# A row's addition ahead of the squares of the row above, the last group's first rows in pairs, and layer 3's second root first: three reorderings in a three-layer network

## The chip, the core and the metric

The kernel runs on 1 core of a Trainium2 chip. Its engines work side by side and meet through semaphores: TensorE (PE; PEld is its weight load), VectorE (DVE), ScalarE (ACT), GpSimd (POOL) and SyncE (SP), which here only issues DMAs. The metric is the device time of one execution in microseconds (us), median over runs; lower is better.

## The reference

Three blocks follow one another on a sequence of 1024 positions with 1024 features, all in float32. The change lies where the second block ends and the third begins:

```python
# end of block 2 (its residual stream is h, DEPTH = 1)
n2 = rms_norm(h, ffn_norm_g)
up = causal_depthwise_conv(n2 @ w_ffn_up, ffn_conv_w, ffn_conv_b)   # 2 x 2816 columns
g, val = up[..., :D_FF_2], up[..., D_FF_2:]
h = h + (jax.nn.silu(g) * val) @ w_ffn_down                          # 2816 -> 1024
h = rms_norm(h, final_norm_g)
# start of block 3
z = rmsnorm(x, pre_g) @ w_in                                         # x is that h; z has v, u, gate, q, k, ...
# end of block 3
x + rmsnorm(y, post_g)
```

`rms_norm(x, g)` is x * rsqrt(mean(x^2) + 1e-6) * g over the features. So two norms with two gains stand between the down product and layer 3's input product.

## The kernel before

**Layout.** Features lie on the 128 partitions, in eight rows (chunks) of 128 features; a row is 128 x 1024. The residual stream is `res` (`k.real(m)` is row m of it). Every large product is made in three matmuls per 128x128 weight block and 512 (or 342) columns: high parts, high times low, low times high (lines 263 to 265 in `product`, 296 to 298 in `three`). An operand therefore exists twice, as `x_hi` (rounded by ScalarE) and `x_lo` (the rest, by VectorE).

**Weights.** They come in the order in which TensorE wants them, in tiles of eight blocks (512 KB). Three buffers each: SP loads `w_raw` (a load waits until POOL is done with the tile three back), ScalarE rounds it to `w_hi` (`cast`, up to three tiles ahead of the tiles TensorE is done with; a cast waits for its load and for the buffer), POOL makes `w_lo` in four quarters, each of which counts `w_ready` up. A row of the down product is four blocks with two pieces of 512 columns, 24 matmuls; two rows use up one tile. A layer 3 product is eight blocks, one tile, 48 matmuls.

**Banks.** `claim` gives a product of two pieces one of two pairs of PSUM banks in turn, and TensorE waits until the reader of the product before in that pair has freed it. Banks 4 to 7 hold sums over partitions.

**Layer 2's MLP (`Ffn2`).** Hidden rows j = 0 to 21 are made by VectorE and ScalarE from the up products (two per j) and kept in a ring of five. The down product runs in groups of hidden rows `ks`: two, then five times four. In the last group `ks` is 18 to 21, and hidden row 21 is the last thing made before it. For each of the eight output rows m the kernel does, in the last group:

- TensorE: the product ("down", 5, m), all chunks of piece 0, then all of piece 1;
- VectorE: adds it to row m of `res` (frees the banks);
- ScalarE: two squares of the row, plain and with the gain (`self.square`), both into one pair of buffers (for m = 0 into the running sums `conv` themselves), so that squares m wait for the running sums of m - 1; then `x_hi` of the row;
- VectorE: adds the two squares to the running sums `conv` (`self.total`; in the profile `up_conv`), then makes `x_lo` of the row (`x3_ready`).

VectorE's order is by hand: addition m, sums m, `x_lo` m, addition m + 1. Behind the last row TensorE sums `conv` over the partitions (the moments, four products of float32 into banks 4 to 7).

**Layer 3's start (`Mixer3`).** From the moments come two roots, each of them guessed by ScalarE (`root_guess`: Ln, then Exp, with table loads) and refined by VectorE (`root_newton`: four dependent operations): `rms`, of layer 2's final norm, and `rms2`, of layer 3's norm, which is then multiplied by `rms`. VectorE's order in `dve` is: first root, two operations for the second root's input (`scale_ready`), eight scalings of `res` by the final gain and `rms` (`x_scaled`), second root, and then the products. ScalarE starts the second guess after the first scaled row. SP's order in `sp`: one small load, wait for eight `x_scaled`, the spill of `res` to DRAM (4 MB; block 3 needs it at its end), wait for it, two loads of 512 KB into the room of `res`, then the next weight tiles. The products v3 0 to v3 7 (values of the spatial gate) run on TensorE right behind the moments; VectorE multiplies each by `rms2` into `mix` (`dve_products`), which frees the banks. Every such multiplication stands behind the wait for the spill. ScalarE applies Gelu to each, and VectorE adds each to a running total one product later (`dve_v_total`), which waits for that Gelu. Six tiles of layer 3 are loaded before SP reaches the wait for the scalings; the first one behind the spill is that of v3 6.

The profile names helper lines: L96 is `tt` (two tensors), L102 `ts`, L105 `stt` (tensor, scalar, tensor), L124 `act`, L129 `copy` (casts), L136 `mm`, L140 `dma`. `work` holds the roots, `mix` the v3 products.

Of the kernel before, what the change touches and what calls it, by code (L numbers as in the profile page):

```python
# [7 lines left out]
P = 128  # L8
S = 1024
# [8 lines left out]
BLOCKS = 8  # L18
# [141 lines left out]
def halves_of(t):  # L160
    return t.rearrange("p (a b) -> p a b", a=2)
# [1844 lines left out]
class Ffn2:  # L2006
# [27 lines left out]
    def pe(self, t):  # L2034
        k = self.k
        for g, (js, ks) in enumerate(self.groups):
            for j in js:
                for i in range(2):
                    drain(k.product(t, ("up", j, i), [block_of("w_ffn_up_2", c, i * FF2 * P + j * P) for c in range(8)], k.hi, k.lo, FFN2,
                                    lambda c, _: [(self.mixer.n_ready, c + 1)]))  # L2040
            for m in range(8):
                drain(k.product(t, ("down", g, m), [block_of("w_ffn_down_2", c, m * P) for c in ks],
                                lambda c: self.h_hi[:, ks[c] % self.RING, :], lambda c: self.h_lo[:, ks[c] % self.RING, :], TWO,
                                lambda c, _: [(self.h_ready, ks[c] + 1)]))
        k.label("ffn 2")
        t.wait_ge(self.total, 14)
        t.mm(k.ones_of(self.conv[:, 0, :], TWO, (4, 5)), self.moments)
        t.mm(k.ones_of(self.conv[:, 1, :], TWO, (6, 7)), self.moments)

    def act(self, a):  # L2050
# [27 lines left out]
    def dve(self, v):  # L2078
# [7 lines left out]
        for g, (js, ks) in enumerate(self.groups):  # L2086
            last = g == len(self.groups) - 1
            for j in js:
# [17 lines left out]
                v.tt(self.h_lo[:, j % self.RING, :], self.conv[:, 0, :], self.h_hi[:, j % self.RING, :].bitcast(F32), ALU.subtract, inc=self.h_ready)  # L2106
            for m in range(8):
                p, x = k.products["down", g, m], k.real(m)
                v.wait_ge(*p.done)
                v.settle()  # L2110
                v.tt(halves_of(x), halves_of(x), k.view(p), ALU.add, inc=p)
                if not last:
                    continue
                v.wait_ge(self.square, 2 * m + 2)
                if m:
                    v.settle()
                    v.tt(self.conv[:, 0, :], self.conv[:, 0, :], self.up[:, 0, 0:S], ALU.add, inc=self.total)
                    v.tt(self.conv[:, 1, :], self.conv[:, 1, :], self.up[:, 1, 0:S], ALU.add, inc=self.total)
                v.wait_ge(self.x3_rounded, m + 1)
                v.stt(k.x_lo[:, m, 0:S], x, self.gains[:, m:m + 1], k.x_hi[:, m, 0:S].bitcast(F32), ALU.mult, ALU.subtract, inc=self.x3_ready)  # L2120


class Mixer3:
# [353 lines left out]
    def act(self, a):  # L2477
# [4 lines left out]
        k.root_guess(a, halves_of(self.rms), ps[:, 4:6, :], D, EPS, self.guess)  # L2482
        a.wait_ge(self.x_scaled, 1)
        k.root_guess(a, self.rms2, self.tmp, D, EPS, self.guess)
# [5 lines left out]
    def dve_products(self, v, name):  # L2490
        k = self.k
        for p in k.since(self.dve_at, name):
            n, i = p.key[0], p.key[-1]
            v.wait_ge(self.spilled, 16)
            v.wait_ge(*p.done)
# [16 lines left out]
            else:  # L2512
                out = self.g[i % 2]
            v.tt(halves_of(out)[rows], k.view(p, rows), halves_of(self.rms2)[rows], ALU.mult, inc=p)
            if n == "v3" and i:
                self.dve_v_total(v, i - 1)

    def dve_v_total(self, v, g):
# [179 lines left out]
    def dve(self, v):  # L2698
# [7 lines left out]
        v.tt(halves_of(self.tmp), ps[:, 6:8, :], halves_of(self.tmp), ALU.mult, inc=self.scale_ready)  # L2706
        for c in range(8):
            v.stt(k.real(c), k.real(c), k.column("final_norm_g_2", c), self.rms, ALU.mult, ALU.mult, inc=self.x_scaled)
        v.wait_ge(self.guess, 2)
# [314 lines left out]
```

## Time and profile before

| | |
|---|---|
| runs | median 3836.55 us of 3 (3836.2 to 3837.43) |
| profiled execution | 3839.78 us, of which the span from first to last instruction is 3838.0 |
| PE | 3533.0 us busy, 92% |
| DVE | 1763.2 us, 46% |
| ACT | 1121.9 us, 29% |
| POOL | 1064.7 us, 28% |
| chain that ended last | PE 80%, DVE 12%, ACT 5%, issue 2% |
| mean granted TensorE clock | 0.955 |

Busy time is summed over the span and can't tell which engine holds up a stage. The chain that ended last is followed back from the last instruction, at each step to what released it. The part of the trace that the change touches lies from about 2750 us (last up product) to about 2930 us (last v3 product) after the span's start.

### The profile page before, as it was taken

What the parts mean: (1) busy time and instruction counts of PE and PEld (TensorE: products, weight loads), DVE (VectorE), ACT (ScalarE), POOL (GpSimd) and SP (SyncE); (2) the same over time, 40 slices, a digit from 0 to 9 for tenths busy, and PEclk for the clock granted to TensorE, in tenths of its full rate; (3) what the DMA queues carried; (4) which work ended last, traced back from release to release, by engine and by line L of the source; (5) the groups of instructions that cost most, each with busy time, mean ns of one, the idle gap of its engine ahead of it and who ended that gap; (6) DMA issues with size and microseconds to landing.
All of it is one profiled execution on the core that took longest, in us unless ns stands there. A gap on an engine that the chain in (4) does not pass through costs nothing.

```text
span 3838.0 us, 39292 instructions
## 1 busy us (share of the span) xinstructions
PE 3533.0 (92%) x16326; PEld 2825.7 (74%) x16326; DVE 1763.2 (46%) x1823; ACT 1121.9 (29%) x1429; POOL 1064.7 (28%) x1136
## 2 busy tenths in 40 slices
PE   8988889999999688999998999999969899999987
PEld 6555667888887488555498989988856777777776
DVE  4566553222222668566456545544553322433433
ACT  3333242111112522434432111111232422322442
POOL 4111334323223233100023334433322122112243
PEclk9999999999999889899799999999989999999999
DMA  3000211111111111000021111111121111000232
GB/s 115 25 22 28 93 61 61 45 49 50 45 50 46 66 61 39 17 6 6 6 78 42 41 50 44 46 48 50 39 83 39 50 63 47 28 28 28 72 131 93
DMA packets 55961, 191.17 MB, mean 50 GB/s; under 512 B 6868, under 2 KB 7252, under 8 KB 55272
## 3 DMA queue, kind: packets, MB, share of 16 engines
q1 hardware_dynamic: 55784, 188.66, 14.5%
q8 instruction: 129, 2.11, 0.2%
q14 instruction: 48, 0.39, 0.0%
HBM read 171.78 MB, written 16.86 MB: 49 GB/s over the span
## 4 chain that ended last, share of the span: by engine, by line
PE 80%; DVE 12%; ACT 5%; issue 2%; DMA 0%; SPq 0%; DVEq 0%; ACTq 0%; POOL 0%; POOLq 0%
PE psum L263 21%; PE psum L265 21%; PE psum L264 21%; PE psum L136 13%; DVE work L96 2%; DVE res L96 2%; DVE res L105 1%; PE psum L296 1%; DVE mix L105 1%; ACT L124 1%; PE psum L298 1%; PE psum L297 1%; ACT res L124 1%; DVE work L114 1%; DVE u_padded L96 1%
## 5 line engine op out<-in xcount | busy, mean ns | idle before, releaser
L96 POOL TENSOR_TENSOR w_lo<-w_raw,w_hi 128x256 fp32r<-128x256 f32 x1132 | 1064.5, 971 | 2738.3 <-ACT w_hi L129 2738.3
L263 PE MATMUL psum<-x_hi,w_hi 128*128 128x512 f32 (+2 forms) x3416 | 1291.1, 378 | 76.9 <-DVE x_lo L96 22.4
L264 PE MATMUL psum<-x_lo,w_hi 128*128 128x512 f32 (+2 forms) x3416 | 1240.1, 363 | 0.0
L265 PE MATMUL psum<-x_hi,w_lo 128*128 128x512 f32 (+2 forms) x3416 | 1237.4, 362 | 0.0
L263 PEld LDWEIGHTS psum<-x_hi,w_hi 128*128 128x128 f32 x3416 | 651.1, 191 | 195.8 <-issue 55.7
L129 ACT CAST w_hi<-w_raw 128x1024 fp32r<-128x1024 f32 x283 | 296.8, 1050 | 1685.8 <-PE psum L265 1640.8
L264 PEld LDWEIGHTS psum<-x_lo,w_hi 128*128 128x128 f32 x3416 | 652.5, 191 | 95.1 <-issue 21.1
L265 PEld LDWEIGHTS psum<-x_hi,w_lo 128*128 128x128 f32 x3416 | 650.0, 190 | 82.6
L263 PE MATMUL psum<-h_hi,w_hi 128*128 128x512 f32 x864 | 345.8, 400 | 31.5 <-issue 10.4
L265 PE MATMUL psum<-h_hi,w_lo 128*128 128x512 f32 x864 | 343.6, 398 | 0.0
L264 PE MATMUL psum<-h_lo,w_hi 128*128 128x512 f32 x864 | 341.4, 395 | 0.0
L263 PEld LDWEIGHTS psum<-h_hi,w_hi 128*128 128x128 f32 x864 | 163.7, 190 | 75.5 <-issue 14.4
L105 DVE SCALAR_TENSOR_TENSOR res<-res,psum 128x1024 f32<-128x1024 f32 (+1 forms) x88 | 90.4, 1027 | 262.0 <-PE psum L265 248.1
L264 PEld LDWEIGHTS psum<-h_lo,w_hi 128*128 128x128 f32 x864 | 164.0, 190 | 40.3 <-issue 2.2
L265 PEld LDWEIGHTS psum<-h_hi,w_lo 128*128 128x128 f32 x864 | 163.9, 190 | 36.6
L136 PE MATMUL psum<-res 128*65 128x256 f32 (+5 forms) x480 | 179.1, 460 | 3.4 <-ACT work L124 3.1
L96 DVE TENSOR_TENSOR h_tmp<-h_tmp 128x1024 f32<-128x1024 f32 (+1 forms) x36 | 54.7, 1521 | 256.1 <-ACT h_tmp L124 256.1
L105 DVE SCALAR_TENSOR_TENSOR mix<-u_padded,vectors,mix 128x1044 f32<-128x1044 f32 x120 | 168.9, 1407 | 5.4 <-ACT work L129 1.2
L96 DVE TENSOR_TENSOR up<-psum,ffn_rms 128x1026 f32<-128x1026 f32 x44 | 54.0, 1227 | 201.6 <-PE psum L265 201.6
L105 DVE SCALAR_TENSOR_TENSOR up_conv<-up,vectors,up_conv 128x1024 f32<-128x1024 f32 x88 | 144.5, 1643 | 3.1
L96 DVE TENSOR_TENSOR res<-res,psum 128x1024 f32<-128x1024 f32 (+1 forms) x56 | 68.5, 1224 | 151.8 <-PE psum L265 150.4
L124 ACT ACT_TABLE_LOAD x100 | 128.3, 1283 | 7.2 <-PE psum L136 5.4
(254 smaller groups left out, 3432.8 us busy)
## 6 DMA issues: line engine op xcount, KB each, us to landing
w_raw<-w_dram SPq DMA_DIRECT2D x283, 512.0 KB, 3.3
res<-spill SPq DMA_DIRECT2D x4, 1044.0 KB, 8.7
res<-x_dram SPq DMA_DIRECT2D x8, 512.0 KB, 8.7
res<-x_dram SPq DMA_DIRECT2D x4, 1024.0 KB, 8.2
spill<-res SPq DMA_DIRECT2D x1, 4096.0 KB, 12.1
spill_a<-mix SPq DMA_DIRECT2D x8, 512.0 KB, 2.6
res<-spill_a SPq DMA_DIRECT2D x8, 512.0 KB, 4.9
x_plain<-spill SPq DMA_DIRECT2D x4, 1024.0 KB, 9.4
```

What stands on the lines that cost most here:

```text
L96: self.mark(self.e.tensor_tensor(out, a, b, op), inc)
L105: self.mark(self.e.scalar_tensor_tensor(out, a, s, b, op0, op1), inc)
L114: self.mark(self.e.reciprocal(out, a), inc)
L124: self.mark(self.e.activation(out, a, func, bias=bias, scale=scale), inc)
L129: self.mark(self.e.copy(out, a), inc)
L136: ins = self.e.matmul(out, lhsT, rhs, start=start, stop=stop, skip_group_check=True)
L263: t.e.matmul(out, whi, xhi, start=k == 0, stop=False, skip_group_check=True)
L264: t.e.matmul(out, whi, xlo, start=False, stop=False, skip_group_check=True)
L265: ins = t.e.matmul(out, wlo, xhi, start=False, stop=last_k, skip_group_check=True)
L296: t.e.matmul(out, whi, xhi, start=first, stop=False, skip_group_check=True)
L297: t.e.matmul(out, whi, xlo, start=False, stop=False, skip_group_check=True)
L298: return t.e.matmul(out, wlo, xhi, start=False, stop=last, skip_group_check=True)
```

## The change

In the last group of the down product rows 0 and 1 are computed together: chunks 18, 19 and 20 of row 0, the same of row 1, then chunk 21 of row 0 and of row 1, each block with both pieces; the weight blocks lie in this order in DRAM. VectorE adds row m + 1 to `res` before it waits for the squares of row m. In layer 3, ScalarE's second guess waits for its input only, not for the first scaled row; VectorE does four scalings, then the second root, then the products; scalings 4 to 7 follow the multiplications of v3 0 to 3, and the multiplications of v3 products don't wait for the spill.

```diff
@@ -2038,7 +2038,10 @@
                 for i in range(2):
                     drain(k.product(t, ("up", j, i), [block_of("w_ffn_up_2", c, i * FF2 * P + j * P) for c in range(8)], k.hi, k.lo, FFN2,
                                     lambda c, _: [(self.mixer.n_ready, c + 1)]))
-            for m in range(8):
+            last = g == len(self.groups) - 1
+            if last:
+                self.pe_first_two(t, g, ks)
+            for m in range(2 if last else 0, 8):
                 drain(k.product(t, ("down", g, m), [block_of("w_ffn_down_2", c, m * P) for c in ks],
                                 lambda c: self.h_hi[:, ks[c] % self.RING, :], lambda c: self.h_lo[:, ks[c] % self.RING, :], TWO,
                                 lambda c, _: [(self.h_ready, ks[c] + 1)]))
@@ -2046,6 +2049,27 @@
         t.wait_ge(self.total, 14)
         t.mm(k.ones_of(self.conv[:, 0, :], TWO, (4, 5)), self.moments)
         t.mm(k.ones_of(self.conv[:, 1, :], TWO, (6, 7)), self.moments)
+
+    def pe_first_two(self, t, g, ks):
+
+        k, products = self.k, []
+        tile, at = divmod(len(k.blocks), BLOCKS)
+        assert at == 0
+        order = [(m, c) for m in range(2) for c in range(3)] + [(m, 3) for m in range(2)]
+        k.blocks += [block_of("w_ffn_down_2", ks[c], m * P) for m, c in order]
+        for m in range(2):
+            p, before = k.claim(("down", g, m), 2, 512)
+            for stream, value in before:
+                t.wait_ge(stream, value)
+            products.append(p)
+        for n, (m, c) in enumerate(order):
+            t.wait_ge(k.w_ready, 4 * tile + n // 2 + 1)
+            t.wait_ge(self.h_ready, ks[c] + 1)
+            r, w = ks[c] % self.RING, (k.w_hi[tile % 3][:, n, :], k.w_lo[tile % 3][:, n, :])
+            for i, (t0, cols) in enumerate(TWO):
+                x = self.h_hi[:, r, t0:t0 + cols], self.h_lo[:, r, t0:t0 + cols]
+                ins = k.three(t, k.ps[:, products[m].first + i, :], w, x, c == 0, c == 3)
+            k.close(t, ins, products[m] if c == 3 else None, n == BLOCKS - 1)
 
     def act(self, a):
         k = self.k
@@ -2104,11 +2128,16 @@
                 v.tt(self.conv[:, 0, :], self.conv[:, 0, :], self.conv[:, 1, :], ALU.mult, inc=self.gated)
                 v.wait_ge(self.h_rounded, j + 1)
                 v.tt(self.h_lo[:, j % self.RING, :], self.conv[:, 0, :], self.h_hi[:, j % self.RING, :].bitcast(F32), ALU.subtract, inc=self.h_ready)
-            for m in range(8):
+            def add(m):
                 p, x = k.products["down", g, m], k.real(m)
                 v.wait_ge(*p.done)
                 v.settle()
                 v.tt(halves_of(x), halves_of(x), k.view(p), ALU.add, inc=p)
+
+            add(0)
+            for m in range(8):
+                if m < 7:
+                    add(m + 1)
                 if not last:
                     continue
                 v.wait_ge(self.square, 2 * m + 2)
@@ -2117,7 +2146,8 @@
                     v.tt(self.conv[:, 0, :], self.conv[:, 0, :], self.up[:, 0, 0:S], ALU.add, inc=self.total)
                     v.tt(self.conv[:, 1, :], self.conv[:, 1, :], self.up[:, 1, 0:S], ALU.add, inc=self.total)
                 v.wait_ge(self.x3_rounded, m + 1)
-                v.stt(k.x_lo[:, m, 0:S], x, self.gains[:, m:m + 1], k.x_hi[:, m, 0:S].bitcast(F32), ALU.mult, ALU.subtract, inc=self.x3_ready)
+                v.stt(k.x_lo[:, m, 0:S], k.real(m), self.gains[:, m:m + 1], k.x_hi[:, m, 0:S].bitcast(F32), ALU.mult, ALU.subtract,
+                      inc=self.x3_ready)
 
 
 class Mixer3:
@@ -2480,7 +2510,7 @@
         k.cast(a, k.at["ffn 2"][0])
         a.wait_ge(self.ffn.moments, 2)
         k.root_guess(a, halves_of(self.rms), ps[:, 4:6, :], D, EPS, self.guess)
-        a.wait_ge(self.x_scaled, 1)
+        a.wait_ge(self.scale_ready, 1)
         k.root_guess(a, self.rms2, self.tmp, D, EPS, self.guess)
         self.act_sgu(a)
         self.act_gla(a)
@@ -2491,7 +2521,8 @@
         k = self.k
         for p in k.since(self.dve_at, name):
             n, i = p.key[0], p.key[-1]
-            v.wait_ge(self.spilled, 16)
+            if n != "v3":
+                v.wait_ge(self.spilled, 16)
             v.wait_ge(*p.done)
             v.settle()
             rows = slice(0, 16) if n == "lr" else slice(0, P)
@@ -2512,8 +2543,15 @@
             else:
                 out = self.g[i % 2]
             v.tt(halves_of(out)[rows], k.view(p, rows), halves_of(self.rms2)[rows], ALU.mult, inc=p)
+            if n == "v3" and i < 4:
+                self.dve_normed(v, 4 + i)
             if n == "v3" and i:
                 self.dve_v_total(v, i - 1)
+
+    def dve_normed(self, v, c):
+
+        x = self.k.real(c)
+        v.stt(x, x, self.k.column("final_norm_g_2", c), self.rms, ALU.mult, ALU.mult, inc=self.x_scaled)
 
     def dve_v_total(self, v, g):
 
@@ -2704,8 +2742,8 @@
         v.tt(self.tmp, self.rms, self.rms, ALU.mult)
         v.settle()
         v.tt(halves_of(self.tmp), ps[:, 6:8, :], halves_of(self.tmp), ALU.mult, inc=self.scale_ready)
-        for c in range(8):
-            v.stt(k.real(c), k.real(c), k.column("final_norm_g_2", c), self.rms, ALU.mult, ALU.mult, inc=self.x_scaled)
+        for c in range(4):
+            self.dve_normed(v, c)
         v.wait_ge(self.guess, 2)
         v.settle()
         k.root_newton(v, self.rms2, self.W[3], self.tmp, D, EPS)
```

## Rows read from the trace of the kernel before

**Rows 1.** Waits of PE, whole span: who waited for whom, total, times, longest.
```profile
PE psum L263 <- DVE mix L96: 15.4, 3, 12.7
...
PE psum L136 <- DVE up_conv L96: 13.3, 1, 13.3
```
**Rows 2.** Timeline of PE, last down group: start, duration, what [idle before, releaser].
```profile
2759.16 0.79 PE L263 MATMUL psum<-h_hi,w_hi 128*128 128x512 f32 x1 [6.29 <-DVE h_lo L96]
...
2763.90 0.39 PE L265 MATMUL psum<-h_hi,w_lo 128*128 128x512 f32 x1
...
2775.24 0.39 PE L264 MATMUL psum<-h_lo,w_hi 128*128 128x512 f32 x1
...
2780.68 0.39 PE L264 MATMUL psum<-h_lo,w_hi 128*128 128x512 f32 x1
...
2793.26 0.50 PE L263 MATMUL psum<-h_hi,w_hi 128*128 128x512 f32 x1 [1.32 <-DVE res L96]
...
2819.89 5.56 PE L136 MATMUL psum<-up_conv,ones 128*128 128x512 f32 x8 [13.34 <-DVE up_conv L96]
```
**Rows 3.** Chain that ended last, down rows: start, duration, what.
```profile
2764.32 1.23 DVE res L96
...
2777.38 1.23 DVE res L96
2778.64 2.12 ACT up L124 x2
2780.78 2.36 DVE up_conv L96 x2
2783.14 1.69 DVE x_lo L105
2784.93 1.23 DVE res L96
```
**Rows 4.** Timeline of DVE, layer 3's start.
```profile
2835.92 11.10 DVE L105 SCALAR_TENSOR_TENSOR res<-res,vectors,work 128x1024 f32<-128x1024 f32 x8
2847.13 1.57 DVE L96 TENSOR_TENSOR work<-work 128x1024 f32<-128x1024 f32 x1
...
2850.72 2.48 DVE L96 TENSOR_TENSOR work<-work 128x1024 f32<-128x1024 f32 x2
2859.14 2.55 DVE L96 TENSOR_TENSOR mix<-psum,work 128x1024 f32<-128x1024 f32 x2 [5.93 <-DMA spill<-res]
```
**Rows 5.** DMA issues, 2835 to 2880: count, KB each, us to landing.
```profile
spill<-res SPq DMA_DIRECT2D x1, 4096.0 KB, 12.1
```
**Rows 6.** Stretch 2860.4 to 2865: length, busy (instructions) by engine, PEclk, DMA share, GB/s.
```profile
2860.40:2865.00 4.60, 4.58 (x12) 3.63 (x13) 1.23 (x1) 2.95 (x3) 2.47 (x4) 0.54 0.89 335
```
**Rows 7.** The scalings of `res` by form: duration ns min/median/max, first and last start.
```profile
L105 DVE SCALAR_TENSOR_TENSOR res<-res,vectors,work x8: 1275/1280/1771, 2835.9 to 2845.3; 128x1024 f32<-128x1024 f32 x8
```
**Rows 8.** Timeline of POOL, the tile made during the scalings.
```profile
2841.85 5.77 POOL L96 TENSOR_TENSOR w_lo<-w_raw,w_hi 128x256 fp32r<-128x256 f32 x4 [25.91 <-ACT w_hi L129]
```
**Rows 9.** Timeline of ACT, the second root's Ln and Exp.
```profile
2837.24 1.16 ACT L124 ACTIVATE work<-work,tiny 128x1024 f32<-128x1024 f32 x1 [6.95 <-DVE res L105]
...
2839.70 1.06 ACT L124 ACTIVATE work<-work 128x1024 f32<-128x1024 f32 x1
```
**Rows 10.** Timeline of DVE, two of the v3 multiplications.
```profile
2895.97 1.23 DVE L96 TENSOR_TENSOR mix<-psum,work 128x1024 f32<-128x1024 f32 x1 [8.04 <-PE psum L265]
...
2907.08 1.22 DVE L96 TENSOR_TENSOR mix<-psum,work 128x1024 f32<-128x1024 f32 x1 [8.04 <-PE psum L265]
```
**Rows 11.** Timeline of SP's queue, 2859 to 2960: the first weight loads behind the spill.
```profile
2860.00 99.65 SPq L140 DMA_DIRECT2D w_raw<-w_dram  x9
```
**Rows 12.** Tile `w_raw`, 2840 to 2900: duration ns min/median/max, first and last start; landing.
```profile
L96 POOL TENSOR_TENSOR w_lo<-w_raw,w_hi x19: 724/732/1717, 2841.8 to 2899.6; 128x256 fp32r<-128x256 f32 x19
L129 ACT CAST w_hi<-w_raw x5: 1027/1054/1054, 2840.7 to 2896.0; 128x1024 fp32r<-128x1024 f32 x5
...
DMA to landing us min/median/max: 3.2/3.3/5.5
```

## Prediction

> **What bounds the kernel now.** I read the waits of TensorE first. Of its matmuls' waits over the whole kernel, two large ones lie where the change is: 13.3 us ahead of the moment matmuls (`up_conv`), and 12.7 of the 15.4 us for `mix`, layer 3's first products [rows 1]. A third, 6.29 us for hidden row 21, stands in the timeline [rows 2]. So here TensorE isn't the limit; what VectorE does while it waits is the path.
>
> Then the timeline of TensorE in the last group of the down product. It restarts after the 6.29 us slowly: 14 steps from 2759.16 to 2763.90 take 4.74 us, where 24 steps from 2775.24 to 2780.68 take 5.44, 0.227 each, which would make 3.2 [rows 2]. These are the two levels of TensorE's clock.
>
> Then the chain, row by row [rows 3]. One period is addition (`res`) 2777.38, two squares on ScalarE 2778.64, two running sums (`up_conv`) 2780.78, `x_lo` 2783.14, next addition 2784.93: 7.55 us. No two of these overlap, since on VectorE the next addition stands behind sums that wait for the squares. The first addition is at 2764.32 [rows 3]; the moments start at 2819.89, after 13.34 us of idling [rows 2]. A row of products is 24 matmuls, 5.46 us, so TensorE is faster than the period and waits for banks (1.32 us at 2793.26) [rows 2].
>
> Then layer 3's start on VectorE: eight scalings in 11.10 us from 2835.92, the second root from 2847.13 to 2853.20 (2850.72 + 2.48), then idle until 2859.14, where the releaser is the spill [rows 4], a DMA of 12.1 us that SP issues behind the eighth scaling [rows 5]. Only then is product 0 read and TensorE let on, at 2860.4, again at the slow pace: 12 matmuls in 4.6 us [rows 6].
>
> **Part 1, rows 0 and 1 in pairs.** No matmul is added. Six (row, chunk) blocks need hidden rows 18 to 20 only: 36 matmuls, of which 9 ran before. The other 27 x 0.227 = 6.1 us go into the 6.29 us wait. TensorE still is held until 2759.16, but has hardly idled, so I take the full pace. Row 0 needs 6 more matmuls: last start 2760.30, and by the distance of before from last start to addition (2763.90 to 2764.32) its addition is at 2760.72 [rows 2, 3]. Row 1 follows 6 matmuls later, 2762.1. The price: row 2 takes row 0's banks and waits for addition 0 (1.23) until 2762.0, 0.1 us after row 1's last matmul.
>
> **Part 2, addition m+1 ahead of sums m.** No instruction is added, but the sums and `x_lo` of row m now stand behind VectorE's wait for product m+1, and the squares of row m+1 still wait for the sums of row m. VectorE's share of a row is 1.26 (addition) + 2.36 (sums) + 1.79 (`x_lo` with POOL beside it) = 5.4 us, 4.9 without POOL [rows 3, 7]. Squares and sums are 2.12 + 2.36 = 4.5. ScalarE has the squares, a third pass of about 1.1 and, every second row, a cast of 1.05: 4.3 at most [rows 3, 12]. All are below the 5.46 us of a row of matmuls. So the pace becomes TensorE's: row 2 starts at 2762.0, addition 2 comes at 2767.7, addition 7 at 2795.0. Behind it remain addition 7 (1.26), sums 6 (2.36, to 2798.65), squares 7 (2.12) and sums 7 (2.36): 2803.2. I allow 0.1 for POOL: moments at 2803.3, against 2819.89: **16.6 us**. Bounds: 16.9 with 5.44 per row; 14.9 if POOL slows the sums too (rival 2). TensorE still idles some 8 us ahead of the moments, so I leave them as slow as they are (5.56 us) [rows 2].
>
> Of POOL's part the trace shows that a scaling of 1.28 us becomes 1.77 while a tile of `w_lo` is made [rows 7, 8]. The Trainium skill (SBUF — State Buffer, "Who interferes with whom") says that a VectorE instruction with two SBUF inputs contends with a GpSimd instruction that reads SBUF, and that whichever is first holds the shared interface for its whole instruction. The trace agrees in kind. By the page both sums are exposed as `x_lo` is, and the addition, with one input in PSUM, is not: that is rival 2, and the sum would be 1.7 us smaller.
>
> **Part 3, layer 3.** Clock times are those of before. ScalarE's second guess waited for the first scaled row and starts at 2837.24; now it starts with `scale_ready`, about 2836.0. Its end, 2840.76 before (2839.70 + 1.06), becomes 2839.5 [rows 9], ahead of where VectorE asks for it. VectorE does four scalings at (11.10 - 3 x 1.69) / 5 = 1.2 us each [rows 4, 7], to 2840.8; three of the eight were slowed and lie 1.69 apart. Then the root, 6.07 us as before, to 2846.9. But the tile of POOL, 5.77 us from 2841.85 [rows 8], starts 1.2 us earlier too and now lies beside all of the root: three more operations with two SBUF inputs, at 0.35 to 0.49 each. I take 1.0, between none and 1.5: 2847.9. The multiplication of product 0 no longer waits for the spill and takes 1.23: TensorE goes on at 2849.2 instead of 2860.4: **11.2 us** (10.7 to 12.2). Its own work ended 12.7 before 2860.4 [rows 1], so the gap is 1.5 us. The 1.32 us gap of the down rows was not followed by a slow stretch (from 2793.26 to the next wait the row takes its 5.5 us), so the slow restart goes too: 12 matmuls at 0.227 are 2.7, not 4.6 us, **1.9 us** [rows 2, 6]. If the clock falls all the same, that 1.9 stays.
>
> The other four scalings follow multiplications 0 to 3, where VectorE idles 8.04 us per product [rows 10]: nothing. They hold no bank up: product 2 needs multiplication 0 alone.
>
> **Part 4, SP's queue.** SP holds, in order: the wait for all eight scalings, the spill, the wait for it, two loads of 512 KB, then the weights of product 6, which went out at 2860.00, 0.87 us after the spill had landed [rows 4, 11]. Products come every 11.11 us [rows 10]. From 2849.2 on, product 3 ends at 2871.4, its multiplication and the eighth scaling at 2874.1, the spill lands at 2886.2, the weight load goes out at 2887.0. It is behind two others, so I take the longest of the landings, 5.5 us, not the median of 3.3: 2892.5. Cast 1.05, the first quarter of POOL 0.73, 0.15 of handing over: 2894.4 [rows 12]. TensorE wants it 4 x 11.11 after 2849.2, at 2893.6. So a new stall of **0.8 us**; none with 3.3, 1.8 with POOL held up. Behind the late weights ScalarE's cast also holds up the activation of product 3, and so VectorE's running sum and the multiplication of product 5 by some 3 us, which nobody needs for 8 us more.
>
> **Sum.** 16.6 + 11.2 + 1.9 - 0.8 = 28.9 us. Behind layer 3's first stage everything is released by events that shift along, so all of it should reach the end. The profiled execution took 3839.78 (span 3838.0), so such a one would take 3810.9. The median of the runs is 3836.55, 3.23 lower: **3807.7 us**. About 0.2% (7.7 us) is what a measurement can tell from no change.
>
> **Rivals.**
> 1. As forecast, 3807.7; its own range goes from 3805.4 (16.9 + 12.2 + 2.0, no stall: 31.1) to 3810. Chance 0.62.
> 2. VectorE becomes the bound of the rows. For: 5.4 us is close under 5.46, and if both sums are slowed by 0.45 as `x_lo` is, a row with a POOL tile has 6.3, the mean of the two kinds of row is 5.65, and six rows lose 0.2 each and the tail 0.5: 1.7 us. Against: there is one tile for two rows, and it doesn't cover all operations. With the low end of part 3: 3809 to 3811. Chance 0.14.
> 3. Small gaps cost the clock, and the weights are later. The 1.5 us gap brings the slow pace back (1.9), the stall grows to 3 with 1.5 of slow pace: 3811 to 3814. For: a 6.29 us wait did bring it. Against: 1.32 us didn't [rows 2]. Chance 0.16.
> 4. The change doesn't do what it says in one stage: rows stay at 7.1 to 7.55 us because something else holds the squares (then 3.6 + 12.3 us: 3820.6), or VectorE meets the spill before product 2 (3820). The code shows no such wait. Chance 0.05.
> 5. Slower. SP's queue: product 6 has its weights only behind the spill. Each product by which the eighth scaling comes later adds 11.1 us of stall; the change loses once the stall passes 29.7 us, three products late (33.3 + 0.8: about 3841). For: the queue is one behind another, and 0.8 us short already. Against: the scaling needs only multiplication 3. Chance 0.02. The last 0.01 is for what I don't see.
>
> Range: 3804 to 3814; rivals 4 and 5 are left out of it. Faster by over 0.2% (below 3828.9): 0.97; within: 0.01; slower: 0.02.
>
> **What would show it.** TensorE without a wait over 0.5 us from 2750.5 to the end of down row 7, and at full pace behind hidden row 21; additions 2 to 7 at 5.46 us (5.6 or more: rival 2); moments 16.6 us earlier. Layer 3: first multiplication without a DMA as releaser, TensorE's gap at product 2 near 1.5 us and 0.23 us steps after it (0.43: rival 3); the spill issued after multiplication 3; a gap under 2 us ahead of product 6 with POOL's `w_lo` as its releaser. I am wrong if product 6 starts over 3 us late, or if the shift at the end of layer 3's first stage is not the shift at the end of the kernel.

## The result, and the profile after

The changed kernel takes 3820.55 us (median of 5, 3814.08 to 3821.82), the kernel before in the same comparison 3837.43 (median of 5, 3836.2 to 3849.49). The ratio is 0.994, 95% interval 0.9928 to 0.9952: some 23 us faster, 18 to 28. (The two medians are only 16.9 us apart; a second comparison of the same two kernels, below, has 22.0 by its medians and a ratio of 0.9943.) 28.9 us were forecast, and 3807.7 us with a range up to 3814. The direction was right; the gain forecast was a quarter too large, and the range missed the time.

The profiled execution of the changed kernel took 3814.08 us, with a span of 3812.3 (before 3838.0).

| | before | after |
|---|---|---|
| PE busy | 3533.0 us | 3524.6 us |
| DVE busy | 1763.2 us | 1764.7 us |
| chain that ended last | PE 80%, DVE 12%, ACT 5%, DMA 0% | PE 81%, DVE 11%, ACT 5%, DMA 1% |
| PE, moments <- `up_conv` (longest wait) | 13.3 us | 9.5 us |
| PE, v3 2 <- `mix` | 12.7 us | 1.9 us |
| PE, v3 6 <- POOL `w_lo` | none | 2.9 us |

Clock times of two executions can't be set side by side as they are: VectorE's last reading of an up product, a multiplication that the change doesn't touch, is at 2749.23 in one and at 2746.15 in the other. (The expectations below call it the last addition of an up product; it is the same instruction.) It is the anchor: from here on places are counted from it, as "+". The anchor before, and in the changed kernel:

```profile
2749.23 1.23 DVE L96 TENSOR_TENSOR up<-psum,ffn_rms 128x1026 f32<-128x1026 f32 x1 [5.39 <-PE psum L265]
```
```profile
2746.15 1.23 DVE L96 TENSOR_TENSOR up<-psum,ffn_rms 128x1026 f32<-128x1026 f32 x1 [5.39 <-PE psum L265]
```

With [rows 2, 10] and the rows below, in us:

| place | before | after | gained in all | forecast |
|---|---|---|---|---|
| moments start | +70.66 | +55.40 | 15.3 | 16.6 |
| product v3 2 starts | +111.2 | +84.87 | 26.3 | 27.8 |
| multiplication v3 7 | +180.06 | +157.96 | 22.1 | 28.9 |
| end of the span | +1088.8 | +1066.2 | 22.6 | 28.9 |

The timeline of PE in the changed kernel, each place where it waits in this stretch (answering to rows 2):

```profile
2756.19 0.47 PE L296 MATMUL psum<-h_hi,w_hi 128*128 128x512 f32 x1 [0.27 <-DVE h_lo L96]
...
2801.55 5.31 PE L136 MATMUL psum<-up_conv,ones 128*128 128x512 f32 x8 [9.47 <-DVE up_conv L96]
...
2831.02 0.50 PE L263 MATMUL psum<-x_hi,w_hi 128*128 128x512 f32 x1 [1.90 <-DVE mix L96]
...
2880.17 0.77 PE L263 MATMUL psum<-x_hi,w_hi 128*128 128x512 f32 x1 [2.88 <-POOL w_lo L96]
```

Hidden row 21 costs 0.27 us instead of 6.29, and no wait for banks is left among the down rows. The last line is new: a product held by its weights.

The timeline of DVE for the rows (answering to rows 3): first addition, additions 2 and 4 with the sums behind it, then the tail, which is what is left behind the last addition.

```profile
2757.86 1.22 DVE L96 TENSOR_TENSOR res<-res,psum 128x1024 f32<-128x1024 f32 x1 [1.81 <-PE psum L298]
...
2764.91 1.22 DVE L96 TENSOR_TENSOR res<-res,psum 128x1024 f32<-128x1024 f32 x1 [1.21 <-PE psum L265]
...
2775.82 1.22 DVE L96 TENSOR_TENSOR res<-res,psum 128x1024 f32<-128x1024 f32 x1
2777.15 2.79 DVE L96 TENSOR_TENSOR up_conv<-up_conv,up 128x1024 f32<-128x1024 f32 x2
...
2793.45 2.36 DVE L96 TENSOR_TENSOR up_conv<-up_conv,up 128x1024 f32<-128x1024 f32 x2
...
2798.03 3.46 DVE L96 TENSOR_TENSOR up_conv<-up_conv,up 128x1024 f32<-128x1024 f32 x2 [0.56 <-ACT up L124]
```

Additions come every 5.4 to 5.5 us, TensorE's pace, and the idle time before them shrinks from 1.21 to none: VectorE only just keeps up. The last two sums take 3.46 us where a pair before took 2.36 or 2.79. POOL makes a tile beside them:

```profile
2795.13 5.29 POOL L96 TENSOR_TENSOR w_lo<-w_raw,w_hi 128x256 fp32r<-128x256 f32 x4 [6.52 <-ACT w_hi L129]
```

DVE at layer 3's start (answering to rows 4, 7 and 10): four scalings, the second root (five operations, from 2822.29), multiplication 0, and multiplications 3 and 7.

```profile
2817.32 4.87 DVE L105 SCALAR_TENSOR_TENSOR res<-res,vectors,work 128x1024 f32<-128x1024 f32 x4
2822.29 1.58 DVE L96 TENSOR_TENSOR work<-work 128x1024 f32<-128x1024 f32 x1
2823.91 1.64 DVE L105 SCALAR_TENSOR_TENSOR work<-work 128x1024 f32<-128x1024 f32 x1
2825.59 1.11 DVE L102 TENSOR_SCALAR work<-work 128x1024 f32<-128x1024 f32 x1
2826.73 2.91 DVE L96 TENSOR_TENSOR work<-work 128x1024 f32<-128x1024 f32 x2
2829.74 1.23 DVE L96 TENSOR_TENSOR mix<-psum,work 128x1024 f32<-128x1024 f32 x1
...
2855.12 1.23 DVE L96 TENSOR_TENSOR mix<-psum,work 128x1024 f32<-128x1024 f32 x1 [7.01 <-PE psum L265]
...
2904.11 1.22 DVE L96 TENSOR_TENSOR mix<-psum,work 128x1024 f32<-128x1024 f32 x1 [8.03 <-PE psum L265]
```

The root takes 7.4 us (2822.29 to 2829.64) against 6.07 before. No operation waits for a DMA any more.

The way of the weights of v3 6 in the chain that ended last, spill to first matmul (answering to rows 5, 11 and 12):

```profile
2856.35 1.20 DVE res L105
2857.57 12.95 DMA spill<-res
2870.53 0.35 SPq L140
2870.92 0.43 SPq L140
2871.39 6.69 DMA w_raw<-w_dram
2878.11 1.05 ACT w_hi L129
2879.30 0.73 POOL w_lo L96
2880.17 0.77 PE psum L263
```

In the kernel before this was nobody's path. Here the chain runs from the eighth scaling through SP's queue to TensorE.

Last, stretches of 4 to 5 us behind the two small gaps (busy time and instructions by engine, then PEclk): v3 2 and v3 6.

```profile
2831.00:2836.00 5.00, 4.98 (x15) 3.97 (x16) 3.84 (x3) 3.05 (x3) 2.86 (x3) 0.66 0.00 0
2880.10:2884.10 4.00, 3.93 (x11) 3.16 (x12) 3.75 (x3) 3.79 (x5) 4.00 (x5) 0.60 0.01 4
```

15 matmuls in 5 us, where full pace makes 21 or 22: the granted clock was at its lower level for part of each stretch, after gaps of 1.90 and 2.88 us.

### The profile page after: what moved, and what is told of

The parts are those of the page before. It is cut to its first block, busy times and chain, and to the rows that moved or that the text cites. A ratio compares the mean times of both kernels' runs of the same rounds, so it can differ in the third digit from the quotient of the medians.

```text
span 3812.3 us, 39293 instructions
## 1 busy us (share of the span) xinstructions
PE 3524.6 (92%) x16326; PEld 2821.8 (74%) x16326; DVE 1764.7 (46%) x1823; ACT 1120.4 (29%) x1429; POOL 1068.8 (28%) x1136
## 4 chain that ended last, share of the span: by engine, by line
PE 81%; DVE 11%; ACT 5%; issue 2%; DMA 1%; SPq 0%; POOL 0%; DVEq 0%; ACTq 0%; POOLq 0%
PE psum L263 21%; PE psum L265 21%; PE psum L264 21%; PE psum L136 13%; DVE work L96 3%; DVE res L96 1%; PE psum L296 1%; DVE mix L105 1%; DVE res L105 1%; ACT L124 1%; PE psum L298 1%; PE psum L297 1%; ACT res L124 1%; DVE work L114 1%; DVE u_padded L96 1%
## 5 line engine op out<-in xcount | busy, mean ns | idle before, releaser
L263 PE MATMUL psum<-h_hi,w_hi 128*128 128x512 f32 x848 | 338.3, 399 | 22.1 <-issue 9.0
## 6 DMA issues: line engine op xcount, KB each, us to landing
spill<-res SPq DMA_DIRECT2D x1, 4096.0 KB, 12.9
```

Of the source, the lines that this page charges most:

```text
L263: t.e.matmul(out, whi, xhi, start=k == 0, stop=False, skip_group_check=True)
```

## Experiments

Each edit is on the kernel named ahead of it. Two fences in a row are two views of the same kernel.

The reasons on trial: (a) the rows are bound by VectorE's order, and the two edits there need each other; (b) what is missing from the forecast is late weights, two slow stretches of TensorE and POOL's work beside VectorE; against it, (c) that the gain is lost downstream or in the spread of the runs.

### Pairs alone

On the kernel before, TensorE's side only:

```diff
+            last = g == len(self.groups) - 1
+            if last:
+                self.pe_first_two(t, g, ks)
-            for m in range(8):
+            for m in range(2 if last else 0, 8):
```

> Only rows 0 and 1 of the last down group in pairs; VectorE's order and layer 3 as before. Places are counted from the last addition of an up product (2749.23 in the kernel before), where the moments start at +70.7 us. Theory (VectorE's row period of 7.1 to 7.55 us is the path, TensorE's wait only sets its start): the first addition is 3.5 us earlier, the period stays, moments at +67.2, the whole kernel 3.5 us faster. Rival (TensorE's wait of 6.29 us and its slow restart are on the path): moments 7.5 to 8 us earlier.

Measured: ratio 0.999 (0.9982 to 0.9999). That is 3 to 4 us by ratio and medians. First addition at +11.7 (+15.1 before), and the moments at +67.16. The rows of DVE (anchor, additions 0 and 2 to 4) and PE's line for the moments:

```profile
2746.85 1.23 DVE L96 TENSOR_TENSOR up<-psum,ffn_rms 128x1026 f32<-128x1026 f32 x1 [5.39 <-PE psum L265]
...
2758.55 1.22 DVE L96 TENSOR_TENSOR res<-res,psum 128x1024 f32<-128x1024 f32 x1 [1.80 <-PE psum L298]
...
2771.55 1.22 DVE L96 TENSOR_TENSOR res<-res,psum 128x1024 f32<-128x1024 f32 x1
...
2779.09 1.22 DVE L96 TENSOR_TENSOR res<-res,psum 128x1024 f32<-128x1024 f32 x1
...
2786.13 1.22 DVE L96 TENSOR_TENSOR res<-res,psum 128x1024 f32<-128x1024 f32 x1
```
```profile
2814.01 5.73 PE L136 MATMUL psum<-up_conv,ones 128*128 128x512 f32 x8 [13.33 <-DVE up_conv L96]
```

The period is still 7.0 to 7.5 us and TensorE idles the same 13.33 us at the end. 6.29 us and a slow restart taken from TensorE are worth 3.5 us. Theory as expected; the rival falls.

### Additions ahead alone

On the kernel before, VectorE's side only, the addition being the function `add` of the change:

```diff
+            add(0)
             for m in range(8):
-                p, x = k.products["down", g, m], k.real(m)
-                v.wait_ge(*p.done)
-                v.settle()
-                v.tt(halves_of(x), halves_of(x), k.view(p), ALU.add, inc=p)
+                if m < 7:
+                    add(m + 1)
```

> Only the addition of row m+1 ahead of the squares of row m; rows 0 and 1 one after the other as before, layer 3 as before. Theory (with the additions ahead the rows go at TensorE's 5.46 us and so TensorE's own 6.29 us wait comes onto the path): additions 5.46 us apart from +15.1 on, addition 7 at +53.3, moments some 9.4 behind it at +62.7, 8.0 us earlier than before; 8 us faster in all. So pairs alone (3.5) and this (8.0) make less than both together (15.3 in the profile of the changed kernel). Rival (parts add up independently): 15.3 - 3.5 = 11.8 us earlier, moments at +58.9.

Measured: ratio 0.9986 (0.9978 to 0.9995), 5.4 us by the ratio; in the trace the moments at +62.71, 8.0 us earlier. Anchor and additions 0, 2 and 7 on DVE, then the moments on PE:

```profile
2747.57 1.23 DVE L96 TENSOR_TENSOR up<-psum,ffn_rms 128x1026 f32<-128x1026 f32 x1 [5.39 <-PE psum L265]
...
2762.76 1.22 DVE L96 TENSOR_TENSOR res<-res,psum 128x1024 f32<-128x1024 f32 x1 [5.32 <-PE psum L265]
...
2773.64 1.22 DVE L96 TENSOR_TENSOR res<-res,psum 128x1024 f32<-128x1024 f32 x1 [3.02 <-PE psum L265]
...
2800.85 1.22 DVE L96 TENSOR_TENSOR res<-res,psum 128x1024 f32<-128x1024 f32 x1
```
```profile
2810.28 6.22 PE L136 MATMUL psum<-up_conv,ones 128*128 128x512 f32 x8 [9.47 <-DVE up_conv L96]
```

The pace is TensorE's, so its stall for hidden row 21 now counts in full. Of the 8.0 us at the moments 7.0 are left at multiplication 7 (+173.1), mostly since the moments took 6.22 us here instead of 5.56; the interval of the ratio goes from 2 to 8 us. Pairs 3.5 and this 8.0 make 11.5; both together 15.3. The rival, 11.8 for this part alone, falls.

### Layer 3's part alone

On the kernel before, all of the change's lines in `Mixer3`, of which:

```diff
-        a.wait_ge(self.x_scaled, 1)
+        a.wait_ge(self.scale_ready, 1)
-        for c in range(8):
+        for c in range(4):
```

> Only the part in layer 3: second guess from its input on, four scalings ahead of the second root, four behind multiplications, no wait for the spill at the products. The down rows are those of before. Theory: product v3 2 starts 11 us sooner behind the moments (40.5 us before, 29.5 now), with a gap of 2.2 us and a slow stretch behind it; the spill goes out behind multiplication 3, the weights of v3 6 come 2.9 us late with another slow stretch; so at multiplication 7 only 6.8 us of the 11 are left, and the kernel is 6.8 us faster. Rival (the lateness of the weights comes from the faster rows ahead, which bring SP's queue into play): no stall at v3 6 here, 11 to 12 us faster.

Measured: ratio 0.9979 (0.997 to 0.9988), 8 us by the ratio; v3 2 starts 29.8 us behind the moments' start, multiplication 7 is at +173.9, 6.1 us earlier than before. The weights are late here as well (PE):

```profile
2849.28 0.50 PE L263 MATMUL psum<-x_hi,w_hi 128*128 128x512 f32 x1 [1.88 <-DVE mix L96]
```
```profile
2898.77 0.77 PE L263 MATMUL psum<-x_hi,w_hi 128*128 128x512 f32 x1 [3.19 <-POOL w_lo L96]
```

So the lateness belongs to this part, not to the faster rows ahead of it. The rival falls.

### The changed kernel once more

> The changed kernel once more, unchanged. Theory (runs of one kernel differ by several us through the granted clock in stretches far from the change, while the stretch of the change repeats): from the last addition of an up product to multiplication v3 7 it takes 158.0 us again within 1 us, against 180.1 before; the place of that anchor and the end differ by up to 4 us between executions; ratio to before near 0.994. Rival (the spread arises in the changed stretch, by its small gaps and late weights): the 158.0 us differ by 3 us or more.

Measured: 3819.36 us (median of 5) against 3841.34, ratio 0.9943 (0.9931 to 0.9955). The anchor lies at 2749.07, multiplication 7 at 2906.90: 157.83 us, against 157.96. From the anchor to the end of the span it takes 1066.2 us both times. But the anchor is 2.9 us later in this execution than in the other. So what differs between these two executions lies ahead of the change. By the records of the granted clock TensorE was at its lower level for 208 us ahead of the anchor in the first and for 218 in this one. Up to the anchor kernel before and changed kernel do the same, so they can be compared there too, and PEclk differs by stretch. The same 40 us of the kernel before, and of the changed one (its first execution; the second has 0.87 there as well):

```profile
1870.00:1910.00 40.00, 38.05 (x124) 19.53 (x123) 18.01 (x25) 15.82 (x30) 0.00 (x0) 0.70 0.00 0
```
```profile
1870.00:1910.00 40.00, 36.29 (x139) 19.95 (x140) 18.96 (x27) 16.80 (x34) 0.00 (x0) 0.87 0.00 0
```

The granted clock is 0.70 in one and 0.87 in the other, 124 matmuls against 139. So the clock makes a part of the spread of some us between single executions. It isn't all of it: in the kernel with all scalings early, below, the lower level also took 218 us ahead of the anchor, and the anchor lies at 2751.62. The rival, by which the spread arises in the changed stretch, falls.

### Weights ahead of the spill

On the changed kernel, SP's queue:

```diff
+        k.load(d, k.at["ffn 2"][0] + 3)
         d.wait_ge(self.x_scaled, 8)
```

> The changed kernel, but SP issues the weight loads of v3 6, 7 and the next one ahead of its wait for the eight scalings; the spill and all else stay. Places are counted from the last addition of an up product; in the changed kernel v3 2 starts at +84.9 and multiplication v3 7 at +158.0. Theory (the weights behind the spill cost the stall of 2.9 us ahead of v3 6 and the slow stretch behind it, 1.6 us): no wait for POOL at v3 6, multiplication 7 at +153.5, 4.5 us faster than the changed kernel; the 1.9 us gap at v3 2 stays. Rival (the stall only moves, since the casts or POOL are late on their own): a stall at v3 6 or 7 remains, under 2 us gained.

Measured: 3813.59 us, ratio to before 0.9932 (0.992 to 0.9945). Multiplication 7 at +152.99, and PE has no wait between v3 2 and the end of the v3 products. 5.0 us came back at that place, 4.5 were expected. The edit isn't behind all of the 5.0: the moments took 6.44 us here instead of 5.31, so that v3 2 starts 1.1 us later than in the changed kernel, and the slow stretch behind v3 2, some 1.5 us, didn't come. Both are the clock's: PEclk is 0.57 over these moments and 0.69 over those of the changed kernel. The two kernels that follow have the same difference. Against the changed kernel (0.994 and 0.9943) the ratio is 3 to 4 us better, but the intervals overlap; the end of the span, in this one execution, is at +1065.8, where the changed kernel has +1066.2. What is shown is the place of the products; on the end see "The sum".

```profile
2898.98 1.23 DVE L96 TENSOR_TENSOR mix<-psum,work 128x1024 f32<-128x1024 f32 x1 [8.03 <-PE psum L265]
```

### The v3 6 weights first behind the spill

On the changed kernel, SP's queue behind the wait for the spill:

```diff
+        k.load(d, k.at["ffn 2"][0] + 1)
         d.dma(self.w_s, dram["a_w_s"], self.s_landed)
```

> The changed kernel, but behind the spill SP issues the weights of v3 6 ahead of the two other loads of 512 KB; the spill keeps its place. In the changed kernel those weights land 6.7 us after their issue, of which 5.5 were expected, and the stall ahead of v3 6 is 2.9 us. Theory (the landing is long since two loads of 512 KB stand ahead of it and two more weight loads go out right behind): landed after 3.3 to 4 us, issued 0.9 earlier, so 3.6 to 4.3 us sooner, the stall is gone, no slow stretch there, multiplication v3 7 at +153.4 instead of +158.0. Rival (the landing is long since TensorE and the others are at work beside it, as the spill is 12.9 us here against 12.1): landed after 5 us or more, a stall of 0.5 us or more remains.

Measured: 3808.69 us (median of 4), ratio 0.9922 (0.9905 to 0.9939). SP's queue, then the cast on ACT that waits for the landing:

```profile
2857.33 0.53 SPq L140 DMA_DIRECT2D spill<-res  x1
2870.30 0.35 SPq L140 DMA_DIRECT2D w_raw<-w_dram  x1
```
```profile
2874.52 1.05 ACT L129 CAST w_hi<-w_raw 128x1024 fp32r<-128x1024 f32 x1 [28.42 <-DMA w_raw<-w_dram]
```

4.2 us from issue to the cast instead of 6.7, and 1.3 us earlier out (0.9 by the order, 0.4 since the spill was issued earlier). The stall is gone: multiplication 7 at +152.97. The order of the DMAs in one queue made the landing long. The spill still takes 12.9 us against 12.1, so the rival may hold for that one; for the weights it falls.

### All scalings behind multiplication 0

On the changed kernel, VectorE:

```diff
-            if n == "v3" and i < 4:
-                self.dve_normed(v, 4 + i)
+            if n == "v3" and i == 0:
+                for c in range(4, 8):
+                    self.dve_normed(v, c)
```

> The changed kernel, but all of scalings 4 to 7 follow multiplication v3 0, none the later ones, so that the spill goes out some 19 us earlier. Theory (same as for the weights ahead: only the lateness of the eighth scaling makes the weights late): no stall at v3 6, multiplication 7 at +153.5, 4.5 us faster than the changed kernel. Multiplication 1 comes 3.8 us later, which product 3 needs only 7 us after that. Rival (the delayed multiplication 1 or the spill beside the products costs as much): +156 or later.

Measured: 3810.71 us, ratio 0.9926 (0.9914 to 0.9939). Multiplication 7 at +152.96, no stall at v3 6. The same 5.0 us by a third way, though the spill took 13.8 us here. The v3 6 weights are again third in the queue and landed after 6.0 us; with an early spill nothing waits for them.

### Casts later

On the changed kernel, ScalarE. In layer 3 the cast of ("v3", 0) likewise comes behind the Gelu of that product.

```diff
-                k.cast(a, k.products["down", g, m].tiles)
+                if not last or m < 7:
+                    k.cast(a, k.products["down", g, m].tiles)
...
                     a.act(k.x_hi[:, m, 0:S], x, ACT.Copy, scale=self.gains[:, m:m + 1], inc=self.x3_rounded)
+                    if m == 7:
+                        k.cast(a, k.products["down", g, m].tiles)
```

> The changed kernel, but two weight casts of ScalarE are moved, and with them POOL's work: the cast ahead of the last down row's squares behind them, and the first cast of layer 3 behind the first Gelu. The weights of v3 6 stay late. Theory (POOL beside VectorE makes the last sums 3.46 instead of 2.36 us and the second root 7.4 instead of 5.7): moments at +54.3 instead of +55.4, v3 2 at +82.0 instead of +84.9, its gap 0.2 us and no slow stretch behind it (1.6 us); multiplication 7 at +153.6. Rival (the slow operations come from something else than POOL, or the slow stretch after the gap comes anyway): moments stay at +55.4, or multiplication 7 at +155 or later.

Measured: 3813.67 us, ratio 0.9929 (0.9916 to 0.9943). Moments at +54.27, v3 2 at +82.66, multiplication 7 at +154.43. POOL's tile now runs from 2801.52 to 2805.41, behind the last sums, and the next one only from 2832.36. On DVE the last sums, the root's first operations and multiplication 0:

```profile
2799.43 2.36 DVE L96 TENSOR_TENSOR up_conv<-up_conv,up 128x1024 f32<-128x1024 f32 x2 [1.02 <-ACT up L124]
...
2823.12 1.23 DVE L96 TENSOR_TENSOR work<-work 128x1024 f32<-128x1024 f32 x1
2824.38 1.22 DVE L105 SCALAR_TENSOR_TENSOR work<-work 128x1024 f32<-128x1024 f32 x1
2825.64 0.69 DVE L102 TENSOR_SCALAR work<-work 128x1024 f32<-128x1024 f32 x1
...
2828.96 1.22 DVE L96 TENSOR_TENSOR mix<-psum,work 128x1024 f32<-128x1024 f32 x1
```

The same operations with POOL elsewhere: 2.36 us instead of 3.46, 1.23, 1.22 and 0.69 instead of 1.58, 1.64 and 1.11. The edit moves two casts of ScalarE as well, but in the changed kernel these are over (2794.99 and 2821.91) before the slowed operations begin; what lies beside those is POOL's tile. The gap ahead of v3 2 is 0.28 us, and the 5 us behind it run at a granted clock of 1.00. Multiplication 7 is 0.8 us later than expected: v3 2 came 0.7 us after its expected place, mostly since the moments took 5.84 us instead of 5.31. The stall at v3 6, which this edit leaves alone, is 3.09 us. The theory holds in each of its steps; the rival falls.

### All together

On the kernel with the casts later:

```diff
-        for c in range(4):
+        for c in range(3):
             self.dve_normed(v, c)
...
-            if n == "v3" and i < 4:
-                self.dve_normed(v, 4 + i)
+            if n == "v3" and i == 0:
+                for c in range(3, 8):
+                    self.dve_normed(v, c)
```

> The changed kernel with the two casts moved, three scalings instead of four ahead of the second root, and the other five behind multiplication v3 0. Theory: moments +54.3, no gap at v3 2 (+81.9), no stall at v3 6, no slow stretch in between, multiplication 7 at +148.6, 9.4 us sooner than in the changed kernel; 31 us and a ratio near 0.992 against the kernel before. Rival (the removed gaps come back elsewhere before the end): multiplication 7 as said but the end less than 6 us sooner than in the changed kernel.

Measured: 3804.42 us (median of 4, 3803.58 to 3805.6) against 3840.21, ratio 0.9908 (0.9895 to 0.9922): some 35 us faster than the kernel before, and faster than the changed one. Multiplication 7 at +149.03, the end 1056.6 us behind the anchor, 9.5 less than in the changed kernel. The traces give less than the ratio: 31.0 us at multiplication 7 and 32.2 at the end, against the kernel before; 31 us lie inside the ratio's interval (30 to 40). All waits of PE from 2750 to 2895:

```profile
PE psum L136 <- DVE up_conv L96: 8.4, 1, 8.4
PE psum L296 <- DVE h_lo L96: 0.3, 1, 0.3
```

What was taken out of the stretch reached the end; the rival falls. The only wait left of any size is that for the sums of the last row.

## Why the prediction was wrong

The waits and the path were as forecast. What failed are the sizes of three terms: POOL's 0.1 us in the tail (measured 1.1), the 1.9 us for a slow restart avoided (0.35), and the 0.8 us for the late weights of v3 6 (2.9, and 1.5 of slow clock behind it). Besides, the level from which the time was counted was too low.

**Part 1, right.** TensorE waits 0.27 us for hidden row 21 and runs at full pace behind it; the first addition is at +11.7, forecast +11.5.

**Part 2, right but for the tail.** Rows go at 5.4 to 5.5 us. The step that failed is the allowance of 0.1 us for POOL. The last sums are the only ones on the path, and they fell beside a tile: 3.46 us instead of 2.36. With squares and handing over, moments at +55.4 instead of +54.1, 1.3 us. Moving the cast gave 1.1 of it back. Rival 2 had the mechanism, in a place where it priced 0.5 us. (Its mean of 6.3 and 4.9 us is 5.6, not 5.65, so its own price was 1.3 us, not 1.7; the rows themselves lost nothing.)

**Part 3, the gap right, the clock wrong.** 11.1 us measured (40.5 to 29.5 us behind the moments), 11.2 forecast. The root took 7.4 us where I had 7.1, and the gap 1.90 where I had 1.5. The 1.9 us for a slow restart avoided didn't come: 15 matmuls in 5 us at PEclk 0.66. I had argued from one gap of 1.32 us. The row behind it has one of 1.80 in the kernel before, with no slow stretch either, so the trace before was for the forecast; that it came out otherwise stays without a shown cause. From v3 2's start to multiplication 2 it takes 12.99 us (2831.02 to 2844.01), in the kernel before 13.34: 0.35 gained, 1.5 missing. The two lines of before:

```profile
2860.42 0.79 PE L263 MATMUL psum<-x_hi,w_hi 128*128 128x512 f32 x1 [12.69 <-DVE mix L96]
```
```profile
2873.76 1.23 DVE L96 TENSOR_TENSOR mix<-psum,work 128x1024 f32<-128x1024 f32 x1 [12.07 <-PE psum L265]
```

**Part 4, the mechanism right, the size wrong.** The stall at v3 6 was foreseen as 0.8 us and is 2.88: the spill took 12.95 us instead of 12.1, and the landing 6.69 instead of 5.5. The spill's time came out of a row in which TensorE stood idle. The landing's came out of one in which the next weight load went out 5.4 us later; here two more went out within 1.1 us. Whether these lengthened it is not shown: third in the queue, such a load landed after 6.83 us with one more right behind it (weights ahead) and after 6.03 with two (all scalings early). Shown is the order: first in the queue it landed after 4.2. On top comes the slow stretch behind the stall: multiplication 6 is 12.84 us behind v3 6's start (2880.17 to 2893.01), 1.5 more than in a product at full pace. Together 3.6 us more than forecast. This is rival 3, which I gave 0.16; its own sum, 16.6 + 11.2 - 3 - 1.5, is 23.3 us, and the measured 22.1 lacks of it little more than the tail.

**The sum.** 15.3 + 11.1 + 0.35 - 2.9 - 1.5 is 22.3, and 22.1 is measured at multiplication 7. Of the 6.8 us missing, 1.3 are the tail, 1.5 the clock behind v3 2, 3.6 the weights and the clock behind them; 0.1 is the gap, and 0.3 is in no term.

That everything would reach the end fits: 22.1 us at multiplication 7 and 22.6 at the end of the span. But one pair of executions could have shown something else. From multiplication 7 on all kernels do the same, and yet single executions differ by up to 8 us here, with the time that TensorE's granted clock was at its lower level, in us:

| kernel | multiplication 7 | from there to the end | of this, at the lower level |
|---|---|---|---|
| before | +180.06 | 908.7 | 79 |
| changed | +157.96 | 908.2 | 79 |
| changed, once more | +157.83 | 908.4 | 79 |
| all together | +149.03 | 907.6 | 80 |
| v3 6 weights first | +152.97 | 905.3 | 72 |
| all scalings early | +152.96 | 909.3 | 87 |
| casts later | +154.43 | 911.1 | 85 |
| weights ahead | +152.99 | 912.8 | 94 |

Where that time is equal, the first four, the rest takes equally long within 1.1 us, and a gain at multiplication 7 is a gain at the end. Where it isn't, one profiled execution can't tell. (The three partial kernels: 904.9 with 72, 912.2 and 912.5 with 86.)

**The level.** 6.8 us put the forecast at 3814.5; the median was 3820.55. The rest is mostly the base. I took the median of three runs, 3836.55, for the kernel's time. Later sets of the same kernel had medians of 3837.43, 3841.34 (28 runs from 3834.12 to 3844.65), 3840.21 and 3841.57. With 3841.34 for the base, 22.1 us less is 3819.2, and the second set of the changed kernel has 3819.36. That 3820.55 is also rival 4's time (3820.6) is chance: the rows go at 5.4 to 5.5 us and VectorE doesn't meet the spill, so nothing of rival 4 happened. An absolute range of 10 us had to hold a spread of 10 us between single executions besides the mechanism. The three runs lay within 1.2 us of each other and didn't show it, though the profiled execution, at 3839.78, lay outside all three.

## What to carry to other kernels

When work is taken off the path, look at what was hidden under it: a queue that had 13 us of idle TensorE to catch up has none afterwards, and here its own steps took longer too (12.95 and 6.69 us instead of 12.1 and 5.5). Putting one DMA ahead of two others gave 5.0 us at multiplication 7, some 4.4 of them the stall and the slow stretch behind it, beside 22 for the whole change. Two edits to one loop may be worth more together than apart, since each makes the other's limit the path: 3.5 and 8.0 us became 15.3. And of an operation that shares a resource ask where it falls when the schedule shifts; the last one before a barrier counts in full.

## What the runs showed that I had not expected

**The clock after a gap of 1.8 to 2 us may go either way.** The gap ahead of v3 2 is 1.88 to 1.96 us in six kernels. In three of them (changed, once more, layer 3 alone) a stretch at the lower clock followed; in the other three it didn't. The 5 us behind the gap with the weights ahead, against 15 matmuls above:

```profile
2832.00:2837.00 5.00, 5.00 (x21) 4.05 (x22) 3.83 (x3) 3.03 (x3) 2.89 (x3) 1.00 0.00 0
```

In the three without it the moments had been slower instead, 6.4 to 6.5 us against 5.3 to 5.6, so that v3 2 started 1.1 us later than in the changed kernel. And in the kernel with the pairs alone a gap of 1.79 us among the down rows, where the kernel before has no slow stretch, was followed by one. Another of 1.77 us in the same kernel was not. I can't say from these runs what decides it; both kernels with no gap to speak of (0.28 us, or none) kept the full pace.

**A spill of 4 MB takes 12.1 us with TensorE idle, 12.9 with products running, 13.8 in the kernel in which it goes out some 20 us earlier (13.9 with all together).** What in the neighbourhood slows it was not tried; VectorE, ScalarE and POOL have other work beside it in each case, so the cause is open.

**VectorE's slowing beside POOL has sizes.** Two operands in SBUF: 1.23 became 1.58 and 1.64 us; a pair of sums 2.36, 2.79 or 3.46, by how much of POOL's tile lay beside them. The Trainium skill (SBUF — State Buffer, "Who interferes with whom") says that a VectorE instruction with two SBUF inputs contends with a GpSimd instruction reading SBUF, and that one with at most one SBUF input, outside the modes that use both ports, doesn't. The additions and multiplications from PSUM agree, 1.22 to 1.23 us in each row of these traces. The `tensor_scalar` of 1.11 instead of 0.69 us has one SBUF input; it too was slowed, and was at 0.69 once POOL was moved. The same section names `tensor_scalar` among the operations that can enter such a mode; whether this one did, no run here shows.
